# mLSTM's gated products and values unsplit in fp32, with another order of its projection chunks

## The chip, the cores and the metric

The kernel runs on one core of one Trainium2 chip. The metric is the device time of one execution in microseconds. Three runs of the kernel before took 1535.57, 1536.1 and 1537.43 us; the median is 1536.1.

## The reference

One sequence of 512 tokens with 1024 channels goes through a first block (differential attention and retention), an mLSTM mixer, a SwiGLU feed-forward layer, a windowed attention mixer, a second feed-forward layer and a final norm. Only the mLSTM mixer is touched. It has 4 heads with 128 query/key columns and 256 value columns. For each head and both directions in time it computes, in its form over all 512 keys, the following:

```
proj = h @ w_in                       # q, k, v, output gates, and 16 input/forget gates
D[t,s] = b[t] - b[s] + log_i[s]       # decay of key s seen from query t, -inf outside the triangle
s[t,s] = (q[t].k[s]) * exp(D[t,s] - m[t])
num = s @ v ;  den = max(|sum s|, exp(-m))
h = num / den                         # forward + backward, then a norm over 256 columns
out = h * norm_w * sigmoid(output gates) ;  x = x + out @ w_out
```

## The kernel before

**Split matmuls.** Almost every matmul is done in the type fp32r with both operands split into a high part (a copy that is rounded to fp32r on ScalarE) and a low part (the source minus the high part, on VectorE). `split` does these two. `mm3` (and the three bare `mm` calls of `outp`) sums high by high, high by low and low by high: three matmuls for one product. `mm4` is one matmul in plain fp32, without a split; the kernel before uses it in the attention mixer, on the tiles FP and VF, which are fp32 views of the memory of FR and VV.

**Queues.** The program is written by hand into one queue for each engine (`Queue`). An instruction waits for semaphore counts; each queue runs in order. `weave` mixes two streams: a main one (the projections, then the output projection) and a side one (the heads). It has a rough clock of its own: each `op` has an assumed duration, WHEN keeps when a result should be due, and a stream is advanced when what it needs is due by TensorE's assumed time; of two that are due, the side goes first. A generator that yields None says that it cannot go on until the other has emitted something.

**Weights.** Chunks of 1024 rows by 256 columns come in by DMA from SP's queue into RAW (two buffers), in the order of the list `chunks`, and are split into WH and WL, also two buffers each. `w_use` takes the next chunk and issues the splits of the one behind it. Every chunk of the mixer's input has the same size.

**m_proj, the main stream** (line 1109 on). First the 128 columns of the input and forget gates (24 matmuls of 512 columns). Then for each head hd: the chunk g (output gates, two tiles of 24 matmuls, then a multiply, a sigmoid and a multiply), the chunk v (four tiles of 24 matmuls of 256 columns, brought out by `v_evac` as high and low part), and the chunk qk (two tiles of 24 matmuls, each brought out and split). The values have two slots, so heads 2 and 3 wait for heads 0 and 1 to be done with theirs (`mpv`). After the first tile of head 0 the norm factor is spread over the partitions (`norm_bcast`) and m_gates may begin. When q and k of a head are emitted, `ready["m", hd]` lets the side begin it.

**m_heads, the side stream.** `m_gates` makes the decays: some twenty VectorE and ScalarE steps in a chain with four scans, and then transposes on TensorE and copies at L1093, L1102 and L1103. Then for each head: `rows` (two spreads of 4 transposes), four `part` (scores of one key tile against all queries, three matmuls of 512 columns; for each of two directions an add, an exponential, a multiply with the scores, and the `split` of the product, at L219 and L206), and four `outp` (for one query tile: five key tiles over both directions, three matmuls each of 258, 256 and 258 columns, so 15 matmuls; then the denominators, the sum, a square with row sum, and the power on POOL). `norm` (L223) and `m_turn` (two transposes, and the multiply with the gates G) follow one and two steps later. For head 3 `part` and `outp` run beside `out_proj`, the next piece of the main stream.

**out_proj.** Four chunks; the first two are done together, in the order of the eight row tiles k of the mixed result, as `("mix", k)` becomes ready (two for each head). Each k is split from G, and brings 4 triples of matmuls of 512 columns for those two chunks. The other two chunks follow when all eight are there.

In the trace all fp32r matmuls stand at L231, plain ones of `mm4` at L246, transposes at L254, VectorE's tensor-tensor at L219, tensor-scalar at L223 and L224, scalar-tensor-tensor at L227, ScalarE at L206 to L209.

Of the kernel before, what the change touches and what calls it, by code (L numbers as in the profile page):

```python
# [5 lines left out]
ALU = mybir.AluOpType  # L6
# [150 lines left out]
def blocks_kernel(nc, A, out):  # L157
# [951 lines left out]
    def m_proj():  # L1109
        j, h, l, wt = w_use()  # L1110
        yield from fm_tile(h, l, wt, 0)
        bg, tg = st["pb"], st["pt"]
        w_done[j] = tg
        norm_col()
        vv_free = st["vv_free"]
        for hd in range(4):
            j, h, l, wt = w_use()
            for u in range(2):
                yield from fm_tile(h, l, wt, u * 128)
                b, t = st["pb"], st["pt"]  # L1120
                g = 2 * hd + u
                if hd == 0 and u == 0:
                    norm_bcast()
                    ready["mgate"] = (bg, tg)
                gate_tile(b, t, g, ACT.Sigmoid)
                ready["g", g] = ts(G[:, g, :], G[:, g, :], SM[:, C_MLN + g:C_MLN + g + 1], ALU.mult, ready["g", g], t_sm)
            w_done[j] = t
            j, h, l, wt = w_use()
            toks = []
            s = hd % 2  # L1130
            V = VV[:, :].rearrange("p (s a i n) -> p s a i n", s=2, a=2, i=4)
            if hd < 2:
                for i in range(4):
                    toks.append(copy(V[:, s, 0, i, 256:258], ONE[:, 0:2], t_one, vv_free))
                ready["vone", s] = toks[-4:]
            else:
                while ("mpv", hd - 2) not in ready:
                    yield None
            for i in range(4):
                b, fb = bank.take()  # L1140
                yield from proj_tm(h, l, wt, i, b, fb)
                t = st["pt"]
                toks += v_evac(b, t, V[:, s, 0, i, 0:256], V[:, s, 1, i, 0:256], i, 256,
                               [ready.get(("mpv", hd - 2)), vv_free])
            ready["mv", hd] = toks + ready["vone", s]
            w_done[j] = t
            while len(fr.q) < 4 + st.get("fr_kept", 10):
                yield None
            j, h, l, wt = w_use()
            got = [(fr.take(), fr.take()) for _ in range(2)]  # L1150
            for u in range(2):
                yield from fm_tile(h, l, wt, u * 128)
                b, t = st["pb"], st["pt"]
                (fh, f1), (fl, f2) = got[u]
                if u == 1:

                    t1 = copy(FR[:, fh, :], PS[:, b, :], t, f1)
                    t2 = tt(FR[:, fl, :], PS[:, b, :], FR[:, fh, :].bitcast(F32), ALU.subtract, t1, t, f2)
                    bank.put(b, t1, t2)
                    tk = [t1, t2]  # L1160
                else:
                    f, ff = ft.take()
                    t1 = stt(FT[:, f, :], PS[:, b, :], 128 ** -0.5, RB[:, :], ALU.mult, ALU.mult, t, st["rbt"], ff)
                    bank.put(b, t1)
                    st["rb_read"] = t1
                    tk = split(FT[:, f, :], FR[:, fh, :], FR[:, fl, :], t1, f1, f2)
                    ft.put(f, tk)
                ready["mqk", hd, u] = (fh, fl, tk)
            w_done[j] = t
            ready["m", hd] = True  # L1170
        st["xfree"] = t

    def m_heads():
        yield from m_gates()
        acol, ecol, tcol, ncol, tnm = ready["mg"]
        V = VV[:, :].rearrange("p (s a i n) -> p s a i n", s=2, a=2, i=4)
        H = {}

        def rows(hd):
# [12 lines left out]
        def part(hd, kt):  # L1192


            x = H[hd]
            qh, ql, tq = ready["mqk", hd, 0]
            kh, kl, tk_ = ready["mqk", hd, 1]
            b, fb = bank.take()
            c = slice(kt * 128, kt * 128 + 128)
            t = mm3(PS[:, b, :], (FR[:, kh, c], FR[:, kl, c]), (FR[:, qh, :], FR[:, ql, :]), True, True, tq, tk_, fb)  # L1200
            rd = []
            for d in range(2):
                f, tnb = x["nmb"][d]
# [12 lines left out]
                rd.append(tg)  # L1216
                n = kt if d == 0 else kt + 1
                if n not in x["gt"]:
                    x["gt"][n] = (fr.take(), fr.take())
                    st["fr_kept"] -= 2  # L1220
                (hb, hf), (lb, lf) = x["gt"][n]
                tk = split(FT[:, p, w], FR[:, hb, w], FR[:, lb, w], tg, hf, lf)
                ft.put(p, tk)
                x["gtok"][d, kt] = (hb, lb, tk)
            bank.put(b, rd)
            if kt == 3:
                for d in range(2):
                    ft.put(x["nmb"][d][0], x["nmr"][d])
                for i in (qh, ql, kh, kl):
                    fr.put(i, t)  # L1230

        def outp(hd, i):
            x = H[hd]
            s = hd % 2
            c = slice(i * 128, i * 128 + 128)
            res = []
            for d in range(2):
                b, fb = bank.take()
                ks = range(0, i + 1) if d == 0 else range(i, 4)
                for kt in ks:  # L1240
                    hb, lb, tk = x["gtok"][d, kt]
                    vh, vl = V[:, s, 0, kt, :], V[:, s, 1, kt, 0:256]
# [19 lines left out]
            if i == 3:  # L1262
                ready["mpv", hd] = t
                st["vv_free"] = t
                for a_, b_ in x["gt"].values():
                    fr.put(a_[0], t)
                    fr.put(b_[0], t)
                st["fr_kept"] = 10 if hd < 3 else 0
            return hd, i, f, [t2, tb], pw

        def norm(hd, i, f, t, pw):
# [3 lines left out]
        for hd in range(4):  # L1275
            while ("m", hd) not in ready:
                yield None
            while len(fr.q) < 10:
                yield None
            st["fr_kept"] = 10  # L1280
            rows(hd)
            for i in range(4):
                yield [ready["mqk", hd, 0][2], ready["mqk", hd, 1][2]]
                part(hd, i)
                if i == 1 and o2 is not None:
                    yield o2[3]
                    m_turn(*o2)
                    o2 = norm(*o1)
                if i == 3 and o2 is not None:
                    yield o2[3]  # L1290
                    m_turn(*o2)
                    o1 = o2 = None
            for i in range(4):
                g = H[hd]["gtok"]
                yield [g[d, kt][2] for d in range(2) for kt in (range(0, i + 1) if d == 0 else range(i, 4))]
                n1 = outp(hd, i)
                n2 = norm(*o1) if o1 is not None else None
                if o2 is not None:
                    yield o2[3]
                    m_turn(*o2)  # L1300
                o1, o2 = n1, n2
        n2 = norm(*o1)
        yield o2[3]
        m_turn(*o2)
        yield n2[3]
        m_turn(*n2)
# [412 lines left out]
```

How the kernel before makes its waits and increments, by code:

```python
    def play(self, eng, sems):  # L90
        for need, fn, inc in self.items:
            for k, v in need:
                eng.wait_ge(sems[k], v)
            ins = fn(eng)
            if inc:
                ins.then_inc(sems[inc[0]], inc[1])
# [1493 lines left out]
        @block.sync  # L1590
        def _(e):
            SP.play(e, sems)
            e.wait_ge(sems["out"], 16 * KT)
```

## Time and profile before

| | us |
|---|---|
| median of three runs | 1536.1 |
| the profiled execution | 1534.96 |
| its span, first to last instruction | 1533.2 |
| PE busy | 1459.8 |
| DVE busy | 855.2 |
| ACT busy | 597.9 |
| mean granted TensorE clock | 0.985 |

The span is what the trace covers; the profiled execution's own time is 1.8 us more. PE is TensorE's matmuls, DVE VectorE, ACT ScalarE, POOL GpSimd, SP SyncE. A matmul's record reaches past the time at which the next one starts, so what one matmul costs in a row of them is read from the distance of starts. An idle TensorE is read from the views of waits, and from a stretch's length less its busy time. A granted clock of 1.00 is 2.4 GHz.

### The profile page before, as it was taken

The page shows a single profiled execution, that of the slowest core. Times are in us where ns is not written, and L with a number is a line of the kernel's source. Part 1 is how long each engine was busy: PE and PEld are TensorE (multiplying, and loading weights), DVE is VectorE, ACT ScalarE, POOL GpSimd, SP SyncE. Part 2 cuts the span into 40 slices and gives each one's busy share as a digit, 9 for nine tenths or more (in the row PEclk, how much of TensorE's full clock was granted, in tenths as well). Part 3 has the DMA queues.
Part 4 walks back from the last instruction along what each step waited for, and adds up shares of the span by engine and source line. Part 5 has one row for each costly group of instructions (what it writes and reads, how often), then busy time and mean ns, then how long its engine had stood idle before and what let it go on. Part 6 is the DMA issues. An engine that isn't in the chain of part 4 may idle for free.

```text
span 1533.2 us, 18333 instructions
## 1 busy us (share of the span) xinstructions
PE 1459.8 (95%) x7200; PEld 1195.5 (78%) x7200; DVE 855.2 (56%) x1639; ACT 597.9 (39%) x1074; POOL 37.8 (2%) x43
## 2 busy tenths in 40 slices
PE   7999998998999789999999999999999999999996
PEld 6778795787888568888888887866678888888885
DVE  5677856566676665443344446487755453344433
ACT  5555533354445534232232333366654232222321
POOL 0011000000000000000000000000000000000000
PEclk9999998999999899999999999999999999999998
DMA  6121120041211103322323223210013322322221
GB/s 232 57 83 62 49 83 28 14 136 57 83 56 56 56 28 110 104 82 92 100 104 110 66 103 115 95 56 1 29 31 107 110 76 93 120 86 107 80 83 71
DMA packets 20901, 123.05 MB, mean 80 GB/s; under 512 B 2256, under 2 KB 2896, under 8 KB 9680
## 3 DMA queue, kind: packets, MB, share of 16 engines
q1 hardware_dynamic: 20816, 121.89, 23.3%
q8 instruction: 57, 0.93, 0.3%
q14 instruction: 28, 0.23, 0.0%
HBM read 119.78 MB, written 2.10 MB: 79 GB/s over the span
## 4 chain that ended last, share of the span: by engine, by line
PE 41%; issue 25%; DVE 6%; ACT 4%; DVEq 0%; POOLq 0%; POOL 0%; ACTq 0%
PE PS L231 38%; DVE FT L227 2%; PE PS L254 2%; PE PS L246 1%; ACT FR L206 1%; DVE FR L219 1%; ACT FT L206 1%; ACT WH L206 1%; DVE WL L219 1%; DVE FT L223 0%; DVE FT L219 0%; DVE G L219 0%; DVE SC L224 0%; ACT XH L206 0%; DVE XT L219 0%
## 5 line engine op out<-in xcount | busy, mean ns | idle before, releaser
L231 PE MATMUL PS<-XH,WH 128*128 128x512 f32 x1080 | 427.5, 396 | 0.0
L231 PE MATMUL PS<-XH,WL 128*128 128x512 f32 x1080 | 420.7, 390 | 0.0
L231 PE MATMUL PS<-XL,WH 128*128 128x512 f32 x1080 | 420.7, 390 | 0.0
L231 PE MATMUL PS<-FR,WH 128*128 128x512 f32 x1088 | 342.1, 396 | 15.0 <-DVE FR L219 9.2
L219 DVE TENSOR_TENSOR WL<-RAW,WH 128x1024 fp32r<-128x1024 f32 (+2 forms) x242 | 263.3, 1130 | 137.9 <-ACT WH L206 136.9
L206 ACT ACTIVATE WH<-RAW 128x1024 fp32r<-128x1024 f32 (+2 forms) x242 | 223.8, 973 | 141.2 <-PE PS L231 135.0
L231 PEld LDWEIGHTS PS<-FR,WH 128*128 128x128 f32 x1088 | 203.5, 190 | 63.3 <-issue 9.2
L231 PEld LDWEIGHTS PS<-XH,WH 128*128 128x128 f32 x1080 | 202.8, 188 | 47.9 <-issue 7.5
L231 PEld LDWEIGHTS PS<-XH,WL 128*128 128x128 f32 x1080 | 202.7, 188 | 43.0
L231 PEld LDWEIGHTS PS<-XL,WH 128*128 128x128 f32 x1080 | 202.9, 188 | 40.3 <-issue 0.5
L231 PE MATMUL PS<-FR,WL 128*128 128x512 f32 x544 | 213.6, 393 | 0.0
L206 ACT ACTIVATE FR<-FT 128x512 fp32r<-128x512 f32 (+3 forms) x118 | 69.4, 588 | 350.5 <-DVE FT L219 292.2
L219 DVE TENSOR_TENSOR FT<-PS,RB 128x512 f32<-128x512 f32 x89 | 61.1, 689 | 213.8 <-PE PS L231 200.8
L219 DVE TENSOR_TENSOR FR<-FT,FR 128x512 fp32r<-128x512 f32 (+3 forms) x118 | 75.3, 638 | 85.8 <-ACT FR L206 85.8
L231 PEld LDWEIGHTS PS<-FR,WL 128*128 128x128 f32 x544 | 103.3, 190 | 22.0
L231 PE MATMUL PS<-WH,XH 128*128 128x256 f32 x288 | 83.7, 291 | 11.8 <-DVE XL L227 11.5
L231 PE MATMUL PS<-FR 64*128 64x512 f32 (+3 forms) x384 | 80.9, 378 | 10.2 <-ACT WH L206 5.0
L206 ACT ACTIVATE FT<-FT 128x512 f32<-128x512 f32 (+2 forms) x81 | 40.7, 504 | 125.0 <-DVE FT L219 101.0
L231 PE MATMUL PS<-WL,XH 128*128 128x256 f32 x288 | 82.1, 285 | 0.0
L231 PE MATMUL PS<-WH,XL 128*128 128x256 f32 x288 | 82.0, 285 | 0.0
L231 PEld LDWEIGHTS PS<-FR 64*128 64x128 f32 (+1 forms) x384 | 54.0, 191 | 32.7 <-issue 13.5
L219 POOL TENSOR_TENSOR SC<-SC,MH 128x1 f32<-128x1 f32 (+2 forms) x38 | 37.4, 985 | 1485.7 <-DVE SC L224 1199.7
(113 smaller groups left out, 1278.5 us busy)
## 6 DMA issues: line engine op xcount, KB each, us to landing
RAW<-in_f_in SPq DMA_DIRECT2D x44, 1024.0 KB, 4.9
RAW<-in_w_in SPq DMA_DIRECT2D x13, 1024.0 KB, 4.9
RAW<-in_m_in SPq DMA_DIRECT2D x12, 1024.0 KB, 4.9
RAW<-in_f_oa SPq DMA_DIRECT2D x16, 768.0 KB, 4.4
RAW<-in_f_ob SPq DMA_DIRECT2D x16, 640.0 KB, 3.8
RAW<-in_a_in SPq DMA_DIRECT2D x6, 1024.0 KB, 5.0
RAW<-in_w_out SPq DMA_DIRECT2D x4, 1024.0 KB, 4.9
RAW<-in_m_out SPq DMA_DIRECT2D x4, 1024.0 KB, 4.9
```

The costliest lines, as they stand in the source:

```text
L206: return AC.op(lambda e: e.activation(o, i, f, scale=scale) if accum is None else e.activation(o, i, f, scale=scale, accum_out=accum), *af ...
L219: return q.op(lambda e: e.tensor_tensor(o, a, b, op), *after, us=us)
L227: return DV.op(lambda e: e.scalar_tensor_tensor(out=o, in0=a, scalar=s, in1=b, op0=op0, op1=op1), *after, us=dve_us(o))
L231: f = lambda e: e.matmul(o, l, r, start=start, stop=stop, skip_group_check=True)
L246: f = lambda e: e.matmul(o, l, r, start=start, stop=stop, skip_group_check=True)
L254: f = lambda e: e.transpose(o, i, ident)
```

## The change

It does five things in the mLSTM mixer:

- the product of scores and decays goes in one VectorE instruction into an fp32 buffer (FP); its split is gone, and a head takes 5 buffers where it took 10;
- the values are brought out once, in fp32 (VF), by ScalarE, and each head has a slot of its own; the columns of ones are set by one memset;
- each product by values is one plain fp32 matmul of 258 columns (`mm4`) where it was three in fp32r;
- the chunks come in the order q0 v0 q1 v1 g0 q2 v2 g1 q3 v3 g2 g3, where it was g0 v0 q0 g1 v1 q1 g2 v2 q2 g3 v3 q3; `norm_bcast` follows the first tile of q0;
- `m_turn` waits, before its transposes, until the output gates of its head are emitted.

```diff
-    for c in range(12):
-        chunks.append((A["m_in"][c], 8, 256))
+    M_ORDER = ("q0", "v0", "q1", "v1", "g0", "q2", "v2", "g1", "q3", "v3", "g2", "g3")
+    for c in M_ORDER:
+        chunks.append((A["m_in"][3 * int(c[1]) + "gvq".index(c[0])], 8, 256))
...
+        V = VF[:, :].rearrange("p (s i n) -> p s i n", s=4, i=4)
+        tv = DV.op(lambda e: e.memset(V[:, :, :, 256:258], 1.0), vv_free)
+        for c in M_ORDER:
+            hd = int(c[1])
+            if c[0] == "g":
...
+                    gate_tile(b, t, g, ACT.Sigmoid)
...
+            if c[0] == "v":
+                j, h, l, wt = w_use()
+                toks = [tv]
                 for i in range(4):
-                toks += v_evac(b, t, V[:, s, 0, i, 0:256], V[:, s, 1, i, 0:256], i, 256,
-                               [ready.get(("mpv", hd - 2)), vv_free])
+                    t1 = copy(V[:, hd, i, 0:256], PS[:, b, 0:256], t, st["rct"], vv_free, scale=st["rc"][:, i:i + 1])
...
+                ready["m", hd] = True
...
-            while len(fr.q) < 4 + st.get("fr_kept", 10):
+            while len(fr.q) < 4 + st.get("fr_kept", 5):
...
-                tg = stt(FT[:, p, w], FT[:, p, w], st["rc"][:, kt:kt + 1], PS[:, b, w], ALU.mult, ALU.mult, te, t, st["rct"])
-                (hb, hf), (lb, lf) = x["gt"][n]
-                tk = split(FT[:, p, w], FR[:, hb, w], FR[:, lb, w], tg, hf, lf)
+                gb, gf = x["gt"][n]
+                tg = stt(FP[:, gb, w], FT[:, p, w], st["rc"][:, kt:kt + 1], PS[:, b, w], ALU.mult, ALU.mult, te, t, st["rct"], gf)
...
-                    mm(PS[:, b, 0:258], FR[:, hb, c], vh, kt == ks[0], False, tk, ready["mv", hd], fb)
-                    mm(PS[:, b, 0:256], FR[:, hb, c], vl, False, False)
-                    t = mm(PS[:, b, 0:258], FR[:, lb, c], vh, False, kt == ks[-1])
+                    gb, tk = x["gtok"][d, kt]
+                    t = mm4(PS[:, b, 0:258], FP[:, gb, c], V[:, hd, kt, :], kt == ks[0], kt == ks[-1], tk, ready["mv", hd], fb)
...
     def m_turn(hd, i, f, tok):
+        while ("g", 2 * hd + 1) not in ready:
+            yield None
+        yield tok
         b, fb = bank.take()
```

## Rows read from the trace of the kernel before

**Rows 1.** The page, part 1: each engine's busy time, share and instructions.
```profile
PE 1459.8 (95%) x7200; PEld 1195.5 (78%) x7200; DVE 855.2 (56%) x1639; ACT 597.9 (39%) x1074; POOL 37.8 (2%) x43
```

**Rows 2.** Seven stretches of the mLSTM: length, busy time (instructions) per engine, granted clock, DMA.
```profile
329.30:357.80 28.50, 28.50 (x174) 25.50 (x172) 20.54 (x29) 16.02 (x23) 0.00 (x0) 1.00 0.27 93
357.80:370.40 12.60, 7.68 (x34) 6.16 (x33) 7.54 (x13) 5.83 (x10) 0.00 (x0) 0.73 0.24 83
370.40:411.20 40.80, 40.49 (x254) 36.56 (x253) 27.80 (x75) 17.73 (x42) 2.30 (x4) 1.00 0.15 52
411.20:459.30 48.10, 46.00 (x281) 40.25 (x280) 32.56 (x84) 23.23 (x47) 2.26 (x4) 1.00 0.19 64
459.30:508.30 49.00, 46.15 (x282) 40.23 (x280) 33.76 (x86) 23.76 (x48) 2.28 (x5) 1.00 0.20 65
508.30:537.10 28.80, 18.61 (x73) 14.07 (x72) 17.98 (x36) 15.98 (x33) 0.00 (x0) 0.82 0.12 42
537.10:556.50 19.40, 13.38 (x87) 11.21 (x86) 12.97 (x48) 4.23 (x12) 2.28 (x4) 1.00 0.00 1
```

**Rows 3.** TensorE's waits, 508.3 to 556.6 us: total, times, longest.
```profile
PE PS L254 <- DVE FT L223: 8.2, 3, 4.9
PE PS L231 <- DVE FR L219: 4.2, 4, 1.7
PE PS L231 <- DVE FT L227: 2.2, 1, 2.2
```

**Rows 4.** TensorE's waits, 357.8 to 370.4 us.
```profile
PE PS L254 <- DVE SC L1093: 3.8, 1, 3.8
```

**Rows 5.** VectorE in time: a product with its split (start, duration, instruction).
```profile
...
513.95 0.35 DVE L227 SCALAR_TENSOR_TENSOR FT<-FT,SC,CO 128x128 f32<-128x128 f32 x1
515.47 0.75 DVE L227 SCALAR_TENSOR_TENSOR FT<-FT,SC,PS 128x512 f32<-128x512 f32 x1 [1.18 <-ACT FT L206]
516.98 0.69 DVE L219 TENSOR_TENSOR FR<-FT,FR 128x512 fp32r<-128x512 f32 x1 [0.77 <-ACT FR L206]
517.59 0.35 DVE L227 SCALAR_TENSOR_TENSOR FT<-FT,SC,CO 128x128 f32<-128x128 f32 x1
```

**Rows 6.** Groups by form: splits of products, values' low parts, table loads (busy us, mean ns).
```profile
L219 DVE TENSOR_TENSOR FR<-FT,FR 128x512 fp32r<-128x512 f32 x94 | 65.1, 693 | 72.5 <-ACT FR L206 72.5
L206 ACT ACTIVATE FR<-FT 128x512 fp32r<-128x512 f32 x94 | 59.4, 632 | 337.3 <-DVE FT L219 292.2 <-DVE FT L227 45.1
L227 DVE SCALAR_TENSOR_TENSOR VV<-PS,SC,VV 128x256 fp32r<-128x256 f32 x32 | 14.6, 481 | 16.7 <-ACT VV L206 16.7
L206 ACT ACT_TABLE_LOAD x17 | 21.8, 1283 | 1.0 <-PEq L1710 0.7
L206 ACT ACTIVATE FR<-FT 128x128 fp32r<-128x128 f32 x8 | 2.5, 310 | 3.3 <-DVE FT L227 3.3
L219 DVE TENSOR_TENSOR FR<-FT,FR 128x128 fp32r<-128x128 f32 x8 | 2.3, 292 | 3.6 <-ACT FR L206 3.6
```

**Rows 7.** TensorE in time: fifteen matmuls of products by values, and what follows.
```profile
434.39 1.98 PE L231 MATMUL PS<-VV,FR 128*128 128x258 f32 x15
436.20 0.28 PE L231 MATMUL PS<-WH,XH 128*128 128x256 f32 x1
```

**Rows 8.** TensorE in time, attention: one plain fp32 matmul, two records, and what follows.
```profile
1025.70 1.02 PE L231 MATMUL PS<-FT,CO 128*128 128x512 f32 x2
1026.65 0.97 PE L231 MATMUL PS<-FR 64*128 64x256 f32 x6
```

**Rows 9.** TensorE in time: output projection, third matmuls of successive triples.
```profile
...
527.58 0.63 PE L231 MATMUL PS<-FR,WL 128*128 128x512 f32 x1
...
528.86 0.63 PE L231 MATMUL PS<-FR,WL 128*128 128x512 f32 x1
...
530.77 0.39 PE L231 MATMUL PS<-FR,WL 128*128 128x512 f32 x1
...
531.46 0.39 PE L231 MATMUL PS<-FR,WL 128*128 128x512 f32 x1
```

More of the change, by code:

```diff
@@ L1115, in m_proj @@
         vv_free = st["vv_free"]
[L1116 to L1132, printed above, removed]
-                for i in range(4):
[L1134 to L1142, printed above, removed]
-                toks += v_evac(b, t, V[:, s, 0, i, 0:256], V[:, s, 1, i, 0:256], i, 256,
-                               [ready.get(("mpv", hd - 2)), vv_free])
-            ready["mv", hd] = toks + ready["vone", s]
-            w_done[j] = t
-            while len(fr.q) < 4 + st.get("fr_kept", 10):
@@ new lines, in m_proj @@
+        V = VF[:, :].rearrange("p (s i n) -> p s i n", s=4, i=4)
[4 more added lines that the diff above has]
+                j, h, l, wt = w_use()
+                for u in range(2):
+                    yield from fm_tile(h, l, wt, u * 128)
+                    b, t = st["pb"], st["pt"]
+                    g = 2 * hd + u
+                    gate_tile(b, t, g, ACT.Sigmoid)
+                    ready["g", g] = ts(G[:, g, :], G[:, g, :], SM[:, C_MLN + g:C_MLN + g + 1], ALU.mult, ready["g", g], t_sm)
+                w_done[j] = t
+                continue
+            if c[0] == "v":
+                j, h, l, wt = w_use()
+                toks = [tv]
+                for i in range(4):
+                    b, fb = bank.take()
+                    yield from proj_tm(h, l, wt, i, b, fb)
+                    t = st["pt"]
+                    t1 = copy(V[:, hd, i, 0:256], PS[:, b, 0:256], t, st["rct"], vv_free, scale=st["rc"][:, i:i + 1])
+                    bank.put(b, t1)
+                    toks.append(t1)
+                ready["mv", hd] = toks
+                w_done[j] = t
+                ready["m", hd] = True
+                continue
+            while len(fr.q) < 4 + st.get("fr_kept", 5):
@@ L1153, in m_proj @@
                 b, t = st["pb"], st["pt"]
+                if hd == 0 and u == 0:
+                    norm_bcast()
+                    ready["mgate"] = (bg, tg)
                 (fh, f1), (fl, f2) = got[u]
@@ L1169, in m_proj @@
             w_done[j] = t
-            ready["m", hd] = True
         st["xfree"] = t
@@ L1175, in m_heads @@
         acol, ecol, tcol, ncol, tnm = ready["mg"]
-        V = VV[:, :].rearrange("p (s a i n) -> p s a i n", s=2, a=2, i=4)
+        V = VF[:, :].rearrange("p (s i n) -> p s i n", s=4, i=4)
         H = {}
@@ L1214, in part @@
                 w = slice(128 * kt, 512) if d == 0 else slice(0, 128 * kt + 128)
-                tg = stt(FT[:, p, w], FT[:, p, w], st["rc"][:, kt:kt + 1], PS[:, b, w], ALU.mult, ALU.mult, te, t, st["rct"])
-                rd.append(tg)
                 n = kt if d == 0 else kt + 1
                 if n not in x["gt"]:
-                    x["gt"][n] = (fr.take(), fr.take())
-                    st["fr_kept"] -= 2
-                (hb, hf), (lb, lf) = x["gt"][n]
-                tk = split(FT[:, p, w], FR[:, hb, w], FR[:, lb, w], tg, hf, lf)
-                ft.put(p, tk)
-                x["gtok"][d, kt] = (hb, lb, tk)
+                    x["gt"][n] = fr.take()
+                    st["fr_kept"] -= 1
+                gb, gf = x["gt"][n]
+                tg = stt(FP[:, gb, w], FT[:, p, w], st["rc"][:, kt:kt + 1], PS[:, b, w], ALU.mult, ALU.mult, te, t, st["rct"], gf)
+                rd.append(tg)
+                ft.put(p, tg)
+                x["gtok"][d, kt] = (gb, tg)
             bank.put(b, rd)
@@ L1233, in outp @@
             x = H[hd]
-            s = hd % 2
             c = slice(i * 128, i * 128 + 128)
@@ L1240, in outp @@
                 for kt in ks:
-                    hb, lb, tk = x["gtok"][d, kt]
-                    vh, vl = V[:, s, 0, kt, :], V[:, s, 1, kt, 0:256]
-                    mm(PS[:, b, 0:258], FR[:, hb, c], vh, kt == ks[0], False, tk, ready["mv", hd], fb)
-                    mm(PS[:, b, 0:256], FR[:, hb, c], vl, False, False)
-                    t = mm(PS[:, b, 0:258], FR[:, lb, c], vh, False, kt == ks[-1])
+                    gb, tk = x["gtok"][d, kt]
+                    t = mm4(PS[:, b, 0:258], FP[:, gb, c], V[:, hd, kt, :], kt == ks[0], kt == ks[-1], tk, ready["mv", hd], fb)
                 dn, rn, ng = sc(), sc(), sc()
@@ L1264, in outp @@
                 st["vv_free"] = t
-                for a_, b_ in x["gt"].values():
+                for a_ in x["gt"].values():
                     fr.put(a_[0], t)
-                    fr.put(b_[0], t)
-                st["fr_kept"] = 10 if hd < 3 else 0
+                st["fr_kept"] = 5 if hd < 3 else 0
             return hd, i, f, [t2, tb], pw
@@ L1277, in m_heads @@
                 yield None
-            while len(fr.q) < 10:
+            while len(fr.q) < 5:
                 yield None
-            st["fr_kept"] = 10
+            st["fr_kept"] = 5
             rows(hd)
@@ L1285, in m_heads @@
                 if i == 1 and o2 is not None:
-                    yield o2[3]
-                    m_turn(*o2)
+                    yield from m_turn(*o2)
                     o2 = norm(*o1)
                 if i == 3 and o2 is not None:
-                    yield o2[3]
-                    m_turn(*o2)
+                    yield from m_turn(*o2)
                     o1 = o2 = None
@@ L1294, in m_heads @@
                 g = H[hd]["gtok"]
-                yield [g[d, kt][2] for d in range(2) for kt in (range(0, i + 1) if d == 0 else range(i, 4))]
+                yield [g[d, kt][1] for d in range(2) for kt in (range(0, i + 1) if d == 0 else range(i, 4))]
                 n1 = outp(hd, i)
@@ L1298, in m_heads @@
                 if o2 is not None:
-                    yield o2[3]
-                    m_turn(*o2)
+                    yield from m_turn(*o2)
                 o1, o2 = n1, n2
         n2 = norm(*o1)
[L1303 to L1306, printed above, removed]
+        yield from m_turn(*o2)
+        yield from m_turn(*n2)
     def m_turn(hd, i, f, tok):
+        while ("g", 2 * hd + 1) not in ready:
+            yield None
+        yield tok
         b, fb = bank.take()
```

## The prediction

> **What bounds the kernel now.** The page first: TensorE is busy for 1459.8 of 1533.2 us, VectorE for 855.2, ScalarE for 597.9 [rows 1]. So matmul time that is added is paid in full wherever TensorE has no gap, and VectorE or ScalarE work that is removed pays only where TensorE stands waiting for it. The change lives in one stage, so the page's shares don't price it; I cut the mLSTM, from its first spread of the norm factor (329.3 us) to the point from which the output projection runs without a stop (556.5), into stretches [rows 2]. Length less busy time gives the gaps: 0.0; 4.9 (357.8 to 370.4, the first head's start); 0.3; 2.1; 2.9 (three times one head beside the next chunks); 10.2 and 6.0 (from 508.3, where only head 3 and the output projection are left). That is 26.4 us in all, 16.2 of it in the tail. Two stretches also have a granted clock of 0.73 and 0.82. In the second the projection's triples start 1.28 us apart (527.58 to 528.86) where at full clock they start 0.69 apart (530.77 to 531.46) [rows 9]; four triples at the low level make about 2.4 us. At the start the 12 matmuls of head 0's scores, four triples too, lie in a stretch whose 0.73 means the low level of 1.2 GHz for about half of it; I put 1.9 of the 2.4 on it. So 26.4 + 4.3 = 30.7 us is the most that any relief of the other engines can give back.
>
> What the gaps wait for: in the tail VectorE's L223 (the normalised head before its transposes, 8.2 us in three waits, the longest 4.9), L219 (the mixed result's split, 4.2) and L227 (2.2) [rows 3]; at the start the copy at L1093 (3.8) [rows 4]. VectorE is not full there (18.0 of 28.8 us [rows 2]); it is a serial chain. [rows 5] show it: the add at 513.95, a wait for the exponential, the multiply at 515.47 that ends at 516.22, a wait of 0.77 for the high copy on ScalarE, the low part at 516.98, and only at 517.59 the next direction's add. A normalise step queued behind this waits for all of it.
>
> **The change, part by part.**
>
> *Products by values.* Before, 15 matmuls take 436.20 - 434.39 = 1.81 us [rows 7], for each of 16 query tiles (4 heads by 4): 29.0 us. After, 5 plain ones. The nearest row is the attention's rotation, one plain fp32 matmul of 512 columns: two records, 1026.65 - 1025.70 = 0.95 us [rows 8]. Four passes of 512 columns at 2.4 GHz (the clock is granted in full in the head stretches) are 0.853 us, so it goes as four passes with 0.10 on top. For 258 columns the passes are 0.430. On top comes at most that 0.10 for each product (0.527), at least nothing (0.430). An fp32r matmul of this size has 1.81/15 - 0.1075 = 0.013 on top, two records would have 0.026, 0.456 in all. Five products stand in a row, so I take 0.456 for each and the 0.10 once: 2.38 us per query tile, 38.1 in all. **TensorE +9.1 us**, bounds +5.4 (0.430) and +13.2 (0.527). The stage has TensorE busy in all but 2 to 3 us of each 49, so this stands on the path.
>
> On the weight loads the Trainium skill speaks against the change: "TensorE: Matmul & The Clock Gate", LDWEIGHTS, gives a load columns/1.2 GHz, 107 ns here, and its section on weight-path perf modes keeps the fast weight load from fp32. If both loads of a product were exposed, an estimate from that page gives 0.43 + 0.21 = 0.64 us for a product and +22 us in all. The attention's 0.10 on top of the passes leaves no room for two such loads, so that row disagrees, and of the chance of rival 2 below only 0.02 is this case (1552).
>
> *The splits.* 32 products (4 heads, 4 key tiles, 2 directions) lose a high copy (ScalarE 632 ns at 512 columns, 310 at 128) and a low part (VectorE 693 and 292) [rows 6]. The widths are 128 to 512 in equal number, so the mean is 0.47 + 0.49 = 0.96 us, and eight are **7.7 us off the serial chain of each head**. For heads 0 to 2 the cover is the next chunks' projection, which has only 5.3 us of gaps left (0.3 + 2.1 + 2.9); as these waits come from the same chain I take 1.3 back, between 0 and 4. For head 3 nothing covers it: the chain stands in the 10.2 us of gaps with the 2.4 of low clock behind them. I take 7.7 there.
>
> *The values' low part.* 16 of the VectorE instructions at 481 ns [rows 6], 7.7 us, and eight tiny copies for one memset. VectorE is busy 33.8 of 49 us in a head's stretch [rows 2] and nobody waits for these at the tiles' pace: nothing. If VectorE were the bound, this would be another gain.
>
> *The order.* Each chunk is of the same size, so SP's loads, the weight splits and the matmuls are the same in number; SP and POOL get nothing more, and the DMA share of the stage is at most 0.27 [rows 2]. What moves: (a) head 0's sigmoids leave the time in which `m_gates` runs. A table load is 1.28 us [rows 6], and sigmoid and exponential alternate there; one or two loads go from its chain. But at the start TensorE waits 3.8 us for a copy [rows 4] which is queued behind other heads' evacuations and a weight split, and that pattern stays. I take 2 of 6.8 (4.9 and 1.9), bounds 0 and 6.8. (b) The chunk g3 comes last. When the transposes of head 2 are let go, TensorE has g3, 16 triples at 0.69 [rows 9] or 11 us, beside head 2's last tiles and the start of head 3, where it had only output projection before. So part of head 3's chain lies beside projection: I take 3 more of the tail. From the tail's 18.6 then come 10.7, and 8 stay: the last products, power, transposes and the split before 556.5 are untouched, and their stretch alone has 6.0.
>
> *The new wait.* `m_turn` stops the side stream until the head's g is emitted. No engine waits for it; TensorE goes on with projection. What is queued behind it is the rest of that head's products and the next head. Its price is that side work is pushed towards the end; priced below.
>
> *The old wait of the values* of heads 2 and 3 for a free slot goes. No wait in the rows is its own: nothing.
>
> Sum: +9.1 - 1.3 - 7.7 - 2 - 3 = -4.9 us, rounded to -5. The profiled execution takes 1534.96, its span 1533.2; it would be 1530. The median of the runs shown is 1.1 above it, so I give 1531.
>
> **The rivals.**
> 1. *Late heads (slower).* With each head's products held until its g, half of head 2's products and all of head 3 come after g2. If `weave` sends g3 ahead of them, its assumed times being shorter than the real chains, half of the product phase stands after the projections. That phase took 19.4 us for one head (the last stretch of [rows 2]), so 9.7 us are added and (b) falls too. If it is half hidden by the output projection it eats 4.9 + 3: then +3 us; unhidden, +8. It decides when less than some 5 us of g3 is left once head 2's first transposes run. For it: `weave` was wrong by 4.9 us in one wait already [rows 3]. Against: of two that are due, the side goes first. 1536 to 1544.
> 2. *The products cost 0.50 or more each (slower or no change).* With the upper bound of +13.2 and the same gains the sum is -0.8. 1535. The row for it is the attention's lone matmul; against it, products here come in fives.
> 3. *All gaps that hang on the chain close (much faster).* 4 in the middle, 6.8 at the start, 14 of the tail, at +7.5 (0.456 flat): -17. For it: chains are the only thing waited for. Against: the last tile's latency and the copy at L1093 aren't touched. 1518.
> 4. *A change of nothing.* The gaps that close are filled by other waits of the same chain (the power on POOL, the square on ScalarE, in the product phase), so that only the 9.1 and some 8 of gains stand: within 2 us of before.
>
> **How the numbers follow.** My forecast -5 with 0.46 (its own range 1524 to 1535), the late heads 0.17, products at their bound 0.11, all gaps 0.14, nothing 0.12. A measurement of this kernel tells about 0.2%, 3 us, from no change. Faster: most of the forecast (0.40) and all gaps, 0.54. Slower: late heads, with 0.04 of dear products, 0.21. Same: 0.25. Range 1517 to 1541: below by rival 3, above by the half hidden rival 1 and beyond.
>
> **What would show it.** Plain products at L246 starting 0.46 to 0.48 us apart in fives, 2.3 to 2.45 us per query tile (wrong above 2.6); no split between a head's multiplies, and a head's score phase some 7 us shorter on VectorE; the wait of 4.9 us for L223 gone; the wait at L1093 still there, 1 to 4 us; TensorE's gaps in the stage at 12 to 17 us instead of 26.4; the granted clock of the tail nearer to 1.00; the point from which the output projection runs unbroken at some 551 us instead of 556.5, and nothing changed after it. Two tiles of g3 lying before head 2's third product tile would show rival 1; a wait that grew at the first spread would break the start's term.

## The result and the profile after

The changed kernel takes **1524.35 us** (median of four runs, 1524.2 to 1526.1) against 1536.4 for the kernel before (four runs). The ratio is 0.9925, 95% interval 0.991 to 0.9939: 12 us faster. Forecast were 1531, a range of 1517 to 1541, and 0.54 for faster. The profiled execution of the changed kernel is the slowest of the four, 1526.1, with a span of 1524.3; the profiled execution before has 1533.2, so this pair differs by only 8.9.

The first part of the page for the changed kernel, to be held against [rows 1]. VectorE has 21 us less to do and ScalarE 17, TensorE 8 more.

```profile
PE 1467.6 (96%) x7120; PEld 1199.6 (79%) x7120; DVE 833.8 (55%) x1592; ACT 581.1 (38%) x1032; POOL 37.8 (2%) x43
```

TensorE's stretches in the changed kernel, cut as in [rows 2] (length, then busy time of PE, PEld, DVE, ACT and POOL, granted clock, DMA share, GB/s): the decays, the start of head 0, its products, two head periods, and the tail in two parts.

```profile
330.90:358.20 27.30, 27.30 (x167) 24.33 (x165) 19.99 (x26) 11.77 (x16) 0.00 (x0) 1.00 0.27 95
358.20:370.10 11.90, 11.90 (x90) 11.04 (x90) 7.16 (x20) 6.66 (x18) 0.00 (x0) 1.00 0.01 2
370.10:395.30 25.20, 25.20 (x137) 22.07 (x137) 14.94 (x40) 10.74 (x20) 1.72 (x3) 1.00 0.24 84
395.30:446.00 50.70, 48.54 (x262) 41.87 (x261) 28.25 (x73) 20.30 (x41) 2.28 (x4) 0.97 0.18 63
446.00:496.80 50.80, 48.63 (x263) 41.97 (x262) 28.31 (x74) 20.37 (x41) 2.29 (x4) 0.97 0.18 63
496.80:514.70 17.90, 15.56 (x74) 12.14 (x72) 12.39 (x33) 9.28 (x21) 0.58 (x1) 1.00 0.17 60
514.70:541.40 26.70, 22.03 (x90) 16.89 (x90) 20.11 (x59) 9.98 (x21) 2.29 (x4) 0.94 0.12 40
```

Length less busy time gives the gaps. The start has 0.0 us of gaps at full clock, where it had 4.9 at 0.73. The two head periods have 2.2 each (before 2.1 and 2.9), now with a dip of the clock. The tail has 2.3 + 4.7 = 7.0 where it had 16.2. From the first spread to the first matmul of the feed-forward layer's norm the stage is 250.5 us against 262.9; its gaps fall from 27.4 to 11.4 us, and TensorE's busy time rises by 3.6. So the stage gains 12.4 us, about the gain of the medians. Outside the stage this pair of executions loses 3.5: it is reached 1.5 us later (330.5 against 328.95), and what follows takes 943.3 us against 941.3, with the same numbers of matmuls but for one record, and ahead of the stage at a slightly lower granted clock (0.97 against 0.98). That stretch of time holds the other 4.3 of the page's 8 us of TensorE. In the other profiles of this document the stage is reached between 328.6 and 331.1 us, whatever the kernel, so this part isn't put down to the change.

TensorE's waits between 370 and 541 us of the changed kernel (total, times, longest), to be held against [rows 3, 4]:

```profile
PE PS L254 <- DVE FT L223: 7.4, 5, 2.2
PE PS L231 <- DVE SC L223: 2.7, 1, 2.7
PE PS L231 <- DVE FR L219: 0.5, 1, 0.5
PE PS L246 <- DVE FP L227: 0.2, 1, 0.2
```

There is no wait for the copy of the decays any more, and the 4.9 us for L223 are gone. A regular wait of 2.2 us for L223 stands at the same place of the scores of heads 1, 2 and 3 (until 408.4, 459.2 and 510.0 us). Behind the first two the clock drops to the low level of 1.2 GHz for eight of the next 18 matmuls; behind the third it doesn't. The stretches behind the first and the third (columns as above; 460.5 to 463.8 us, behind the second, has 0.50 too):

```profile
409.30:412.60 3.30, 3.30 (x10) 2.53 (x9) 2.16 (x7) 1.55 (x5) 0.00 (x0) 0.50 0.00 0
510.00:514.70 4.70, 4.53 (x20) 3.45 (x20) 3.18 (x9) 2.94 (x7) 0.00 (x0) 1.00 0.00 0
```

The products by values, ten records for five plain matmuls of one query tile (start, duration), with what follows, and the ten weight loads (PEld):

```profile
392.87 2.34 PE L246 MATMUL PS<-VF,FP 128*128 128x258 f32 x10
395.05 0.38 PE L254 MATMUL PS<-CO,FT 128*128 128x128 f32 x2
...
392.77 2.04 PEld L246 LDWEIGHTS PS<-VF,FP 128*128 128x128 f32 x10
```

395.05 - 392.87 = 2.18 us, 0.436 for a product, where 15 fp32r matmuls took 1.81 [rows 7]. For 16 query tiles that is 34.9 us against 29.0, +5.9. Four passes of 258 columns at 2.4 GHz are 0.430, so 0.006 is left: the two loads of a product's weights lie beside the matmuls and add nothing that can be seen. The Trainium skill gives a load as columns/1.2 GHz ("TensorE: Matmul & The Clock Gate", LDWEIGHTS) and keeps the fast weight load from fp32 (its section on weight-path perf modes). The prediction's estimate from that page, 0.64 us for a product with both loads exposed, is not what this row shows.

### The profile page after: what moved, and what is told of

It reads as the page before. It is cut to its first block, busy times and chain, and to the rows that moved or that the text cites. A ratio compares the mean times of both kernels' runs of the same rounds, so it can differ in the third digit from the quotient of the medians.

```text
span 1524.3 us, 18003 instructions
## 1 busy us (share of the span) xinstructions
PE 1467.6 (96%) x7120; PEld 1199.6 (79%) x7120; DVE 833.8 (55%) x1592; ACT 581.1 (38%) x1032; POOL 37.8 (2%) x43
## 4 chain that ended last, share of the span: by engine, by line
PE 62%; issue 25%; DVE 8%; ACT 4%; DMA 0%; POOL 0%; DVEq 0%; POOLq 0%; SPq 0%; ACTq 0%
PE PS L231 57%; PE PS L246 3%; PE PS L254 2%; DVE WL L219 1%; DVE FT L227 1%; DVE FT L219 1%; ACT FR L206 1%; DVE FR L219 1%; ACT FT L206 1%; ACT WH L206 1%; DVE G L219 1%; DMA RAW<-in_w_in 0%; DVE FT L223 0%; DVE FP L227 0%; DVE STR L227 0%
## 5 line engine op out<-in xcount | busy, mean ns | idle before, releaser
L219 DVE TENSOR_TENSOR WL<-RAW,WH 128x1024 fp32r<-128x1024 f32 (+2 forms) x242 | 263.2, 1129 | 153.8 <-ACT WH L206 152.9
L206 ACT ACTIVATE FR<-FT 128x512 fp32r<-128x512 f32 x86 | 54.4, 633 | 329.7 <-DVE FT L219 292.5
L219 DVE TENSOR_TENSOR FT<-PS,RB 128x512 f32<-128x512 f32 x89 | 61.1, 689 | 213.7 <-PE PS L231 200.7
L219 DVE TENSOR_TENSOR FR<-FT,FR 128x512 fp32r<-128x512 f32 x86 | 59.6, 693 | 66.1 <-ACT FR L206 66.1
L219 POOL TENSOR_TENSOR SC<-SC,MH 128x1 f32<-128x1 f32 (+2 forms) x38 | 37.5, 987 | 1476.7 <-DVE SC L224 1215.7
```

The source lines that it names most:

```text
L206: return AC.op(lambda e: e.activation(o, i, f, scale=scale) if accum is None else e.activation(o, i, f, scale=scale, accum_out=accum), *af ...
L219: return q.op(lambda e: e.tensor_tensor(o, a, b, op), *after, us=us)
```

## Experiments

Each run has its own kernel before beside it on the same chip, at 1535.65 (runs 1 to 4), 1536.7 (5 to 8), 1536.4 (9 to 11) and 1536.1 (12). Ratios are against that one, with the 95% interval in brackets. Where two runs of different groups are held against each other, these kernels before differ by up to 1 us, and the four times of one kernel lie 2 to 5 us apart, so a difference below some 3 us isn't told from none.

**1. The order alone.** The arithmetic of before in the new order, with the wait in `m_turn`.

```diff
-    for c in range(12):
-        chunks.append((A["m_in"][c], 8, 256))
+    M_ORDER = ("q0", "v0", "q1", "v1", "g0", "q2", "v2", "g1", "q3", "v3", "g2", "g3")
...
+        while ("g", 2 * hd + 1) not in ready:
+            yield None
```

> The new order of chunks, the late norm spread and the wait of m_turn for its gates, with the arithmetic of before: products and values split, three fp32r matmuls each, two slots for the values. Theory A (two parts that add: the order closes the gaps at the start, the arithmetic shortens the serial chain of each head): the start's 4.9 us of gaps and its low clock go, the wait for the copy at L1093 too, and a part of the tail; 1526 to 1531. Theory B (all of the gain is the arithmetic, which frees VectorE and ScalarE everywhere, also in the start): the gaps at the start stay, 1534 to 1540, or slower because the side stream is held back.

1538.6 us, ratio 1.0015 (1.0006 to 1.0025): 3 us slower. This is theory B's range, and as it said, the start keeps its wait of 3.8 us: the order does not close it. The waits in the tail, between 505 and 560 us, are larger than those of before (17.4 us against the 14.6 of [rows 3]), and the stage's mean granted clock is 0.94 (before 0.97):

```profile
PE PS L254 <- DVE FT L223: 6.5, 2, 6.3
PE PS L231 <- DVE FT L227: 6.3, 2, 3.3
PE PS L231 <- DVE FR L219: 4.6, 2, 3.8
```

That is the direction of rival 1, but not its sign. The sign was that tiles of g3 lie before head 2's third product tile; here all 48 matmuls of g3 come behind the fourth one (which starts at 497.5) and beside head 3's scores, as the forecast's (b) had it. TensorE then stands for 6.3 us before head 2's last transposes and for another 6.3 in head 3's first products, behind the long split chain. Why nothing stands beside them, no run takes apart.

**2. The arithmetic alone.** The changed kernel's unsplit products and values, in the order g v q.

```diff
-    M_ORDER = ("q0", "v0", "q1", "v1", "g0", "q2", "v2", "g1", "q3", "v3", "g2", "g3")
+    M_ORDER = ("g0", "v0", "q0", "g1", "v1", "q1", "g2", "v2", "q2", "g3", "v3", "q3")
```

> The unsplit products and values as in the changed kernel, in the order of before (g v q for each head). Theory A: the plain products cost TensorE 5.9 us more than the fp32r ones (80 at 0.436 against 16 times 1.81), the tail's chain is some 8 us shorter, the start keeps its wait: 1530 to 1535. Theory B: nearly the whole gain is here: 1523 to 1527.

1528.3 us, ratio 0.9954 (0.9939 to 0.9969): 7.3 faster, between the two theories. The start's wait is gone here, in the old order, so it belongs to the arithmetic. With unsplit arithmetic the new order is then worth about 4 us more, of which the two profiles show 2.8 in the stage (253.2 against 250.5 us); with split arithmetic it costs 3. The two parts do not add.

**3. The kernel before without the products' split.** The low part is left out and the third matmul takes the high part again.

```diff
-                tg = stt(FT[:, p, w], ..., te, t, st["rct"])
-                tk = split(FT[:, p, w], FR[:, hb, w], FR[:, lb, w], tg, hf, lf)
+                tk = stt(FR[:, hb, w], ..., te, t, st["rct"], hf, lf)
...
-                    t = mm(PS[:, b, 0:258], FR[:, lb, c], vh, False, kt == ks[-1])
+                    t = mm(PS[:, b, 0:258], FR[:, hb, c], vh, False, kt == ks[-1])
```

> The kernel before, where the product of scores and decays is written once as fp32r; its low part is left out and the third matmul takes the high part again, so TensorE's work is that of before and only the serial chain is shorter. Theory A (the chain is what the tail waits for): 16.2 us of gaps in the tail fall by 7 to 10, 1525 to 1529. Theory B (VectorE and ScalarE are late through their whole load, of which these 32 splits are a third): the gaps fall in the middle too, 1522 to 1525. If neither the chain nor the load decides, within 2 us of before.

1523.5 us, ratio 0.992 (0.9905 to 0.9935): 12.2 faster, at the same work for TensorE. Its start is as before, 3.8 us for L1093. The waits of its tail, against [rows 3]:

```profile
PE PS L231 <- DVE FR L219: 4.4, 4, 1.7
PE PS L254 <- DVE FT L223: 3.1, 2, 2.0
PE PS L231 <- DVE FR L227: 0.8, 1, 0.8
```

They are 8.3 us in these rows and were 14.6; the 2.4 us of low clock behind the longest went too. The gaps of the middle (371 to 505.7 us) fall only from 5.3 to 3.4 us, so most of the gain is the tail's, though the time is in theory B's range. Leaving out the splits is the largest part of the gain. How much of it is the shorter chain itself is not shown: the planner's sum lost the splits too and mixed the streams otherwise (between head 2's last transposes and head 3's first three query tiles stand 24 matmuls of the output projection, where there were 42), and no run leaves out the splits and keeps every queue's order.

**4. The new order without the products' split.** As run 3, in the new order.

> The new order with the values split and three fp32r matmuls for each product, of which the low part is left out as in the run before this one. Against the changed kernel it has 5.9 us less of TensorE work and the values' low part more. Theory A: what TensorE saves is paid out in full where it has no gap, so 4 to 6 us faster than the changed kernel, 1518 to 1521. Rival: the stage's end hangs on the heads' chain, so TensorE's cheaper products only turn into gaps: 1523 to 1525.

1525.7 us, 0.9933 (0.9917 to 0.995), outside both forecasts. That is 2 us above run 3 and 1.4 above the changed kernel, neither clear of the noise; but the 4 to 6 us that its cheaper products were to bring against the changed kernel are not there. What stands against them is the values' low part, and with it the wait of 3.8 us at the start: the stage has 15.9 us of gaps, 4.9 of them there, against 11.4.

**5. The kernel before without the values' low part**, the second matmul taking the high part again.

```diff
-                toks += v_evac(b, t, V[:, s, 0, i, 0:256], V[:, s, 1, i, 0:256], i, 256, ...)
+                t1 = copy(V[:, s, 0, i, 0:256], PS[:, b, 0:256], t, st["rct"], ...)
...
-                    mm(PS[:, b, 0:256], FR[:, hb, c], vl, False, False)
+                    mm(PS[:, b, 0:256], FR[:, hb, c], vh[:, 0:256], False, False)
```

> The kernel before, whose values are only rounded to fp32r: their low part is left out (16 VectorE instructions of 0.48 us gone), and the second matmul takes the high part again, so TensorE does the same work. The prediction said that nobody waits for these: 1534 to 1537. Theory C, from the runs so far, where the start's wait of 3.8 us is there whenever the values have a low part and gone when they don't: the gaps of the start go with them, 4.9 us and the low clock, 1528 to 1531.

1529.9 us, 0.9961 (0.9947 to 0.9975): 6.8 faster, as theory C had it, from 16 instructions for which TensorE waits 0.4 us in all in the kernel before (for VV at L227, between 370 and 508 us). The gain is the start's: its 4.9 us of gaps and its low clock are gone, while the waits of the tail are those of [rows 3] to the digit.

**6. The same, with every engine's order kept.** The 16 instructions stay, one column wide; the planner counts them as 256.

```diff
-                toks += v_evac(b, t, V[:, s, 0, i, 0:256], V[:, s, 1, i, 0:256], i, 256, ...)
+                t2 = DV.op(... out=V[:, s, 1, i, 0:1] ..., us=0.07 + 0.00104 * 256)
```

> As the run before this one, but the 16 instructions stay in their places with one column in place of 256 (0.15 us in place of 0.48), and the planner counts them as before, so that every engine's order is word for word that of the kernel before. Theory C1 (the start gains because VectorE's queue is planned otherwise: two scans of the decay chain come before a weight split and the copy at L1093 before another): the wait for L1093 stays, 1534 to 1536. Theory C2 (the start gains because VectorE has 1.3 us less to do there): as fast as the run before this one.

1535.3 us, 0.9993 (0.9983 to 1.0002): not told apart from the kernel before, and at most 2.6 us below it. Its wait at the start is unchanged:

```profile
PE PS L254 <- DVE SC L1093: 3.8, 1, 3.8
```

TensorE's, VectorE's and ScalarE's instructions stand in the same order as in the kernel before, so what run 5 gains is not, or to the smaller part, the time of these instructions; it is the order that the planner makes without them. VectorE in time, kernel before, around the start (WL is the second half of a weight split, SCAN a step of the decay chain, L1093 the copy that TensorE waits for):

```profile
...
348.10 2.36 DVE L219 TENSOR_TENSOR WL<-RAW,WH 128x1024 fp32r<-128x1024 f32 x2 [0.53 <-ACT WH L206]
350.49 1.21 DVE L1074 TENSOR_TENSOR_SCAN FT<-ONE,FT 32x512 f32<-32x512 f32 x1
351.73 1.22 DVE L1076 TENSOR_TENSOR_SCAN FT<-ONE,FT 32x512 f32<-32x512 f32 x1
...
357.00 1.21 DVE L1081 TENSOR_TENSOR_SCAN FT<-FT 32x512 f32<-32x512 f32 x1
...
360.45 0.69 DVE L219 TENSOR_TENSOR FR<-PS,FR 128x512 fp32r<-128x512 f32 x1 [1.18 <-ACT FR L206]
361.46 2.36 DVE L219 TENSOR_TENSOR WL<-RAW,WH 128x1024 fp32r<-128x1024 f32 x2 [0.32 <-ACT WH L206]
363.74 0.42 DVE L1093 COPY SC<-PS 128x256 f32<-128x256 f32 x1
```

And in run 5:

```profile
...
345.09 1.21 DVE L1074 TENSOR_TENSOR_SCAN FT<-ONE,FT 32x512 f32<-32x512 f32 x1
346.33 1.22 DVE L1076 TENSOR_TENSOR_SCAN FT<-ONE,FT 32x512 f32<-32x512 f32 x1
348.48 2.36 DVE L219 TENSOR_TENSOR WL<-RAW,WH 128x1024 fp32r<-128x1024 f32 x2 [0.93 <-ACT WH L206]
...
354.75 1.21 DVE L1081 TENSOR_TENSOR_SCAN FT<-FT 32x512 f32<-32x512 f32 x1
...
357.53 0.42 DVE L1093 COPY SC<-PS 128x256 f32<-128x256 f32 x1 [0.51 <-PE PS L254]
...
359.77 0.69 DVE L219 TENSOR_TENSOR FR<-PS,FR 128x512 fp32r<-128x512 f32 x1 [0.78 <-ACT FR L206]
360.79 2.36 DVE L219 TENSOR_TENSOR WL<-RAW,WH 128x1024 fp32r<-128x1024 f32 x2 [0.33 <-ACT WH L206]
```

Without the low parts in the planner's sum, the two scans are queued ahead of the weight split of 2.36 us, the rest of the chain is earlier, and the copy comes before the k evacuation and the next weight split instead of behind them: 357.5 instead of 363.7 us.

**7. The old order, all in fp32r without low parts.** Runs 3 and 5 together. Of the instructions, run 2 differs from it in the kind of the products by values alone; the mix of the streams differs a little around each head's last product tile.

> The order of before, neither products nor values with a low part, and three fp32r matmuls as before (the second and third take the high parts again). Against the unsplit kernel in the old order (1528.3) it differs in the kind of the products by values alone. If what TensorE does more for plain products is paid in full, it is 5.9 us faster than that one: 1521 to 1524. If the heads' chain hides a part of it, 1524 to 1527.

1518.9 us, 0.9888 (0.9873 to 0.9903), 9.4 less than run 2 and below both forecasts. TensorE's busy time in the stage is 231.7 us against 237.9, 6.2 less, near the 5.9; the gaps are 13.0 against 15.3. The dear products are paid in full, and some 2 us of gaps come with them. The last 0.9 is not in the two stages. It also checks run 5: the kernel of run 3 with the values' low part gone as well gains 17.8 us where it gained 12.2.

**8. The normalise step early**, in the changed kernel. VectorE in time there, in one head period:

```profile
...
407.32 0.48 DVE L227 SCALAR_TENSOR_TENSOR FP<-FT,SC,PS 128x256 f32<-128x256 f32 x1 [0.38 <-ACT FT L206]
407.71 0.42 DVE L219 TENSOR_TENSOR G<-PS,G 128x256 f32<-128x256 f32 x1
408.05 0.34 DVE L223 TENSOR_SCALAR FT<-FT,SC 128x256 f32<-128x256 f32 x1
```

The last product of the second key tile (407.32) is followed by the multiply of one finished query tile and the normalise step of the next (408.05), for which TensorE waits until 408.4. This step needs nothing of these products.

```diff
+                if i == 0 and o2 is not None:
+                    n2 = norm(*o1)
                 part(hd, i)
                 if i == 1 and o2 is not None:
                     yield from m_turn(*o2)
-                    o2 = norm(*o1)
+                    o2 = n2
```

> The changed kernel, where the normalise step of the last query tile of a head is queued on VectorE ahead of the next head's first scores instead of behind its second. In the changed kernel TensorE waits three times 2.2 us for it, and twice runs 18 matmuls at the low clock behind it (about 1.7 us each). If this wait is all that holds TensorE there: 1514 to 1518. If the next item of the same chain is late instead: 1521 to 1524.

1518.9 us, 0.9886 (0.9871 to 0.9901), 5.4 faster than the changed kernel. The three waits are gone and the clock of the stage is 1.00. It lies 0.9 above the first range, and the tail now waits more, 9.3 us from 505 on (7.0 in the changed kernel, 2.2 of them the wait that went):

```profile
PE PS L246 <- DVE FT L223: 3.7, 1, 3.7
PE PS L246 <- DVE FP L227: 2.3, 1, 2.3
PE PS L231 <- DVE FR L219: 2.0, 2, 1.3
PE PS L254 <- DVE FT L223: 1.3, 1, 1.3
```

**9. q v g for each head**, unsplit.

```diff
-    M_ORDER = ("q0", "v0", "q1", "v1", "g0", "q2", "v2", "g1", "q3", "v3", "g2", "g3")
+    M_ORDER = ("q0", "v0", "g0", "q1", "v1", "g1", "q2", "v2", "g2", "q3", "v3", "g3")
```

> The changed kernel with the chunks as q v g for each head, so that no head is held back by its output gates. The changed kernel takes 1524.4, the same arithmetic in the order g v q 1528.3. If holding the heads back costs time (the late heads of the prediction's rivals), this order is faster than the changed one: 1519 to 1522. If keeping g2 and g3 for the end is what the new order gains (projection beside head 3), it is slower: 1526 to 1529.

1525.2 us, 0.9924 (0.9905 to 0.9943): the same as the changed kernel, between the two forecasts. So neither holding the heads back nor keeping two g chunks for the end decides, unless the two cancel. What g v q (run 2) lacks and both have is each head's g behind its q and v, g3 among them.

**10. The early normalise step in the old order.** The edit of run 8 on the kernel of run 2.

> The unsplit kernel in the order g v q (1528.3), with the normalise step queued ahead of the next head's scores. In the new order that edit gave 5.5 us. If the new order and this edit help for separate reasons, the same gain is found here: 1522 to 1524. If the wait that the edit removes is one that the new order made (a head's last transposes now fall beside the next one's scores), there is little to gain: 1526 to 1529.

1529.8 us, 0.9958 (0.9942 to 0.9973), 1.5 above run 2 and not told from it: nothing gained, where the same edit gave 5.4 us in the new order. Between 371 and 505 us TensorE still waits 6.1 us for L223, but in other places. Run 2's waits of 0.9 us behind the scores are gone; those before a head's last product tile have grown from 1.6 to 2.2 us, and nine matmuls run at the low clock behind each (from 433.0 and from 484.1 us), where in run 2 none do.

**11. A more careful plan.** Run 8, the planner's assumed latency from an instruction to its result set from 0.07 to 0.20 us in the mLSTM.

```diff
-        WHEN[self.name, self.n] = self.t + 0.07
+        WHEN[self.name, self.n] = self.t + LAT[0]
...
+    LAT[0] = 0.2
     weave(chain(m_proj(), out_proj(C_FFN0)), m_heads(), PE, bank, soon)
+    LAT[0] = 0.07
```

> The kernel with the early normalise step (1518.9), where the planner assumes each result of the mLSTM 0.13 us later than before (0.20 us behind its instruction and not 0.07); no instruction is changed, only the order in which the two streams are mixed. What is left of TensorE's waits there (1.2 us beside the heads, 9.3 in the tail) comes from results that are later than planned. If the plan is what makes them: 1513 to 1517. If they are the chain itself, with nothing else to put before them: 1518 to 1521.

1514.45 us, 0.9859 (0.9843 to 0.9874): 22 us faster than before and the fastest here. Its stretches until the output projection runs unbroken (columns as above):

```profile
328.90:364.00 35.10, 35.10 (x230) 32.24 (x229) 22.98 (x29) 14.30 (x21) 0.00 (x0) 1.00 0.27 91
364.00:500.00 136.00, 135.98 (x750) 118.52 (x749) 85.24 (x225) 61.85 (x127) 6.85 (x12) 1.00 0.19 67
500.00:531.00 31.00, 24.93 (x106) 19.58 (x105) 22.40 (x64) 11.64 (x26) 2.27 (x4) 0.94 0.10 34
```

There is no gap until 500 us; 6.1 us stay in the tail. It is in the first range: these gaps were made by the plan.

**12. The same plan on the kernel before**, nothing else changed.

> The kernel before, with nothing changed but the planner's assumption (0.20 us in place of 0.07 from an instruction to its result, in the mLSTM alone). On the changed kernel with the early normalise step it gave 4.5 us. If the gaps of the kernel before (26.4 us) are made by its plan as much as by its long chains, a good part closes: 1520 to 1529. If its chains are simply too long for the work that lies beside them, there is nothing to put in the gaps: 1533 to 1537. If the mixing is only moved about by chance, it can be slower.

1543.7 us, 1.0051 (1.0034 to 1.0068): 7.6 us slower. New waits stand in the middle, 371 to 505 us, where the kernel before had 5.3 us of gaps (this kernel's lines are one further down, L220 for L219):

```profile
PE PS L232 <- ACT WH L207: 4.6, 1, 4.6
PE PS L232 <- DVE FR L220: 4.1, 2, 3.6
PE PS L232 <- DVE FT L228: 2.1, 1, 2.1
```

At the start, though, TensorE waits for nothing: the wait of 3.8 us is gone, with every instruction of the kernel before in place. That wait was the plan's, as runs 5 and 6 say. A larger latency is not a better plan as such. It moved the streams against each other, well in one kernel and badly in the other.

## Why the prediction was right, and where not

The time lay in the range, and the direction and its main reason held: TensorE pays for the plain products, and the tail gives back more. The gain was 12 us and not 5, so the size was wrong by more than a factor of two, and the time lies at the very edge of the forecast's own 1524 to 1535. By steps:

- *Products by values*, +9.1 forecast, **+5.9** measured (0.436 for a product, 0.476 taken, bounds 0.430 to 0.527; 2.18 us per query tile, under the 2.3 to 2.45 of the sign). The 0.10 on top of the attention's lone matmul is not met by five in a row; in the trace of [rows 8] its two records start at 1025.70 and 1026.13, so the first takes 0.431 us, hardly more than two passes of 512 columns (0.427), and the 0.10 stands behind the second, before the next kind of matmul. Run 7 shows the price is paid: 9.4 us with the gaps beside it. By the Trainium skill ("FP8 and Floating Point Precision", TensorE Precision Notes) true fp32 takes four passes. The trace agrees: 0.430 of 0.436. The 1552 of the case with exposed loads is a slip: the forecast's gains of 14.0 and a price of 22 make some 1544.
- *The splits in the tail*, -7.7, with -3 for the order. Gaps fell by 9.2 us (16.2 to 7.0), and of the 2.4 us of low clock 1.3 are left (six matmuls of the output projection behind the wait of 2.7 us take 2.7 us, where they take 1.4 at full clock). That is near the forecast. Run 3 gives 12.2 us for leaving out the splits alone where 9 were forecast (7.7 and 1.3), chain and plan together.
- *The values' low part*, forecast at **nothing**: this is the step that failed. It is worth 6.8 us (run 5), and run 6 finds no time of the instructions themselves (1.4 us, an interval that includes nothing and ends at 2.6). The prediction asked who waits for them, and the answer was right but for 0.4 us. It did not ask what the planner does when they leave its sum.
- *The start*, -2 forecast for (a), the sigmoids out of the way, with the wait for L1093 kept. It gave back its 4.9 us of gaps and its low clock, and not by the order: run 1 has the order and the wait, runs 2 and 5 have the old order and no wait. So (a) is worth nothing, and the start's gain is the values' term: with the 1.9 us of low clock it is the 6.8 of the upper bound, reached by another way than (a). "That pattern stays", said of the copy behind an evacuation and a weight split, is the sentence that broke. Its own sign, a wait of 1 to 4 us at L1093, didn't come.
- *The middle*, -1.3: 5.3 us of gaps became 4.3, but the low clock behind two of its waits costs 1.7 us each, so the middle lost some 2 us.
- *The order*, -5 in all by (a) and (b). It is +3.0 with split arithmetic and about -4 with unsplit. Rival 1 said that this could turn out slower, and in run 1 it does, but without its sign (g3 ahead of head 2's products), which isn't in the changed kernel either. Run 9 holds no head back and takes the same time, so no price of holding the heads shows.
- Rivals 2, 3 and 4: the products cost less than their bound, the gaps closed at the start but not in the middle, and no other waits filled them (11.4 us are left, a little under the 12 to 17 of the sign). So none came.

The 7 us beyond the forecast are then 4.8 more at the start and 3.2 less for the products, with 3.7 less in the middle; the rest, some 3 us, is in the tail and in the matmul records that reach into each gap, and isn't split further. The unbroken output projection begins at 541.4 us, well before the 551 of the forecast, but with more of it still to do: from there to the end of the stage it is 39.6 us, against 35.4 before.

What stays open is why the new order is 4 us better with unsplit arithmetic. Run 9 speaks against the length for which the heads wait; where the g chunks stand, g3 above all, is left, but the plan changes with every such edit, and no run kept the plan and moved g3. Nor is it shown for the splits how much is the chain and how much the plan.

## To carry to other kernels

Where a program mixes streams by assumed times, an instruction's cost in that sum can be worth more than its time on the engine: price an edit by what it does to the order of each queue, and to tell the two apart keep the order and shrink the instruction, as run 6 did. In an in-order queue look for a short step that is ready and stands behind a long chain; moving one by two tiles gave 5.4 us here, and nothing in the other order (run 10), so try it in the order that is kept. And two parts of a change are to be run apart and together, since the order was a loss with one arithmetic and a gain with the other.

## What was not expected of the hardware

In the changed kernel a plain fp32 matmul of 258 columns in a row of its kind costs 0.436 us, 1.4% above its four passes, while in the kernel before an fp32r one of 256 or 258 columns costs 0.121 [rows 7], 12% above its one. So a plain one is 3.6 fp32r ones and not 4, and against three for a split product it costs 0.436 to 0.362. The same wait of TensorE, 2.2 us for L223, was followed by the low clock twice and once not. At 408.6 us the next 18 matmuls took 5.8 us where 18 take 4.1: the first two or three ran near full speed, eight ran at half (granted clock 0.50 from 409.3 to 412.6), and the last ones at full speed again. So the 1.7 us are lost by eight matmuls; the expectation of run 8 speaks of 18.
